# Fourth input-projection chunk of a decoder step computed by seven half-sized products, with the vector engine's work around it laid out anew

## What is computed

```
h = rmsnorm(x)
xin, bg, cg, q, k, v, g_conv, g_attn = split(h @ w_in)     # w_in: 1024 x 6400
y_conv = bg * (causal 3-tap convolution of (cg * xin))
y_attn = attention(rmsnorm(q), rmsnorm(k), v, window 128, bias table, sinks)
x = x + (sigmoid(g_conv)*y_conv + sigmoid(g_attn)*y_attn) @ w_out
x = x + mixture_of_experts(rmsnorm(x))    # top 4 of 32 experts, 1024 x 2048 up and 1024 x 1024 down each
```

## Time and profile before

| | us |
|---|---|
| median of three runs | 1146.74 |
| the profiled execution's own time | 1146.49 |
| span of its trace | 1144.7 |
| PE busy | 1096.0 (96% of the span) |
| VectorE (DVE) busy | 441.5 (39%) |
| VectorE busy from 80 to 100 us | 19.24 of 20 |
| PE idle for DMA, all in the expert stage | 39.9 |

### The profile page before, as it was taken

One profiled execution on the slowest core, in us unless ns is written; L12 is line 12 of the kernel. 1 busy time (PEld: TensorE's weight loads), 2 busy tenths in 40 slices (PEclk: granted clock), 3 DMA queues, 4 the chain that ended last, 5 costly groups with the idle time before them and its releaser, 6 DMA issues.

```text
span 1144.7 us, 15230 instructions
## 1 busy us (share of the span) xinstructions
PE 1096.0 (96%) x6125; PEld 503.9 (44%) x6125; DVE 441.5 (39%) x864; ACT 190.5 (17%) x405; POOL 88.7 (8%) x161
## 2 busy tenths in 40 slices
PE   9999999999999999999899999999999999999997
PEld 6889898543333333333333333333333333333333
DVE  6578786652433323233222222323232323232322
ACT  3233341221321101010101010101010101010101
POOL 1775215000000000000000000000000000000000
PEclk9999999999999999999999999999999999999999
DMA  9937529999999999999999999999999999999996
GB/s 317 320 119 212 184 86 370 418 368 416 402 418 435 415 432 430 435 428 435 427 434 434 428 435 428 435 427 435 434 427 436 428 434 428 435 433 429 427 423 270
DMA packets 53206, 444.38 MB, mean 388 GB/s; under 512 B 13100, under 2 KB 19372, under 8 KB 35740
## 3 DMA queue, kind: packets, MB, share of 16 engines
q1 hardware_dynamic: 46712, 435.83, 91.6%
q0 software_dynamic: 5600, 7.32, 2.4%
q10 hardware_dynamic: 852, 0.64, 0.2%
HBM read 439.78 MB, written 2.37 MB: 386 GB/s over the span
## 4 chain that ended last, share of the span: by engine, by line
PE 62%; DMA 37%; DVE 0%; issue 0%; ACT 0%; ACTq 0%; SPq 0%; DVEq 0%
PE pA L2115 33%; DMA ring<-in_w_up 21%; PE pB L2115 20%; DMA ring<-in_w_down 10%; PE pM L2115 6%; DMA area<-in_w_up 5%; PE pM L2118 1%; PE pA L2118 1%; DMA x<-in_x_prompt 1%; ACT area L1327 0%; DVE x L1961 0%; SPq L848 0%; DVE conv_row L1875 0%; DVE x L2042 0%; ACTq L1109 0%
## 5 line engine op out<-in xcount | busy, mean ns | idle before, releaser
L2115 PE MATMUL pA<-ring,hn 128*64 128x512 f32 x1536 | 352.7, 602 | 23.9 <-DMA ring<-in_w_up 23.8
L2115 PEld LDWEIGHTS pA<-ring,hn 128*64 128x64 f32 x1536 | 105.3, 137 | 219.5 <-issue 185.4
L2115 PE MATMUL pB<-ring,area 128*64 128x512 f32 (+3 forms) x784 | 169.2, 582 | 6.5 <-DMA ring<-in_w_down 5.7
L2115 PE MATMUL pA<-area,hn 128*64 128x512 f32 x512 | 119.3, 609 | 10.4 <-DMA area<-in_w_up 10.4
L2115 PE MATMUL pB<-area,ring 128*128 128x132 f32 (+3 forms) x896 | 119.6, 313 | 0.6 <-DVE tmp L1453 0.5
L2115 PEld LDWEIGHTS pB<-area,ring 128*128 128x128 f32 (+1 forms) x896 | 105.0, 179 | 14.1 <-issue 2.5
L2115 PEld LDWEIGHTS pB<-ring,area 128*64 128x64 f32 (+2 forms) x784 | 58.8, 136 | 98.3 <-issue 85.9
L1961 DVE TENSOR_TENSOR x<-pM,x 128x512 f32<-128x512 f32 x60 | 40.1, 692 | 147.6 <-PE pM L2115 147.6
L1315 ACT ACTIVATE area<-area 128x512 f32<-128x512 f32 x30 | 19.0, 632 | 386.2 <-DVE area L1944 386.2
L1875 DVE COPY conv_row<-pM 128x512 f32<-128x512 f32 x30 | 20.6, 686 | 146.8 <-PE pM L2115 146.8
L2115 PEld LDWEIGHTS pA<-area,hn 128*64 128x64 f32 x512 | 36.0, 139 | 74.5 <-issue 59.5
(11 more groups left out here) (351 smaller groups left out, 918.1 us busy)
## 6 DMA issues: line engine op xcount, KB each, us to landing
ring<-in_w_up SPq DMA_DIRECT2D x36, 4096.0 KB, 29.8
ring<-in_w_down SPq DMA_DIRECT2D x18, 4096.0 KB, 29.2
area<-in_w_up SPq DMA_DIRECT2D x12, 4096.0 KB, 30.2
ring<-in_w_up SPq DMA_DIRECT2D x16, 2048.0 KB, 12.7
area<-in_w_down SPq DMA_DIRECT2D x6, 4096.0 KB, 30.1
ring<-in_w_in SPq DMA_DIRECT2D x22, 1024.0 KB, 9.6
ring<-in_w_down SPq DMA_DIRECT2D x16, 1024.0 KB, 10.2
ring<-in_w_up SPq DMA_DIRECT2D x16, 1024.0 KB, 8.3
```

What stands on the lines that cost most here:

```text
L2115: return pe.matmul(out, w, m, start=start, stop=stop, skip_group_check=True)
```

## The change

Chunk 4 joins `SEVEN`: its four tiles (32 matmuls of 128x264) become seven products (56 matmuls of 128x132). It uses the early activation sums (`EARLY_SIDES`). VectorE gets four more weight sums, and the reads and multiplications of the seven products in place of four tile multiplications; ScalarE one more copy. The multiplication goes into `cx`, with a semaphore of its own, `xin_ready`, for which the first taps wait. The steps around it move: chunk 5's sums stand inside chunk 4, three of them; chunk 6's sums start after slot 5 of chunk 5 and end after slot 2 of chunk 6; unit 0's exponential and scaling stand at slots 0 and 4 of chunk 4; the sample's `s_norm` after slot 6 of chunk 4, its `s_turn` and `s_values` two steps later than before (slots 5 of chunk 5 and 0 of chunk 6); the first four `taps` steps, before at tiles 16 and 17 and twice at slot 0 of chunk 5, stand at slots 0, 0, 1 and 3 of chunk 5; the transpose of the cached keys (`cache_cols`) stands at slot 2 of chunk 2. With one more entry in `RING`, chunks 5, 6 and 7 are loaded one chunk later.

```
-SEVEN = (2, 3, 5, 6, 7, 9, 10, 11, 12)
-EARLY_SIDES = (2, 3, 5)
+SEVEN = (2, 3, 4, 5, 6, 7, 9, 10, 11, 12)
+EARLY_SIDES = (2, 3, 4, 5)
...
-UNIT_STEPS = [(slot(3, 2), slot(3, 4), slot(3, 4), slot(3, 6), slot(3, 6), slot(5, 4), slot(5, 6)),
+UNIT_STEPS = [(slot(3, 2), slot(3, 4), slot(3, 4), slot(4, 0), slot(4, 4), slot(5, 4), slot(5, 6)),
...
-STATE_TAP_STEPS = [14, slot(7, 4)]
-FIRST_TAP_STEPS = [15, 16, 17, 17, 30, 31, 32, 33]
-TAP_STEPS = [16, 17, slot(5, 0), slot(5, 0), 31, 32, 33, slot(9, 0)]
-SIDE_MOVES = [slot(5, 2), slot(5, 4), slot(6, 0)]
+STATE_TAP_STEPS = [slot(4, 4), slot(7, 4)]
+FIRST_TAP_STEPS = [slot(4, 5), slot(4, 5), slot(4, 6), slot(4, 6), 30, 31, 32, 33]
+TAP_STEPS = [slot(5, 0), slot(5, 0), slot(5, 1), slot(5, 3), 31, 32, 33, slot(9, 0)]
+SIDE_MOVES = [slot(5, 2), slot(5, 4), slot(6, 2)]
...
-             5: (14, 15, 17, slot(5, 0)),
-             6: (slot(5, 3), slot(5, 5), slot(6, 0), slot(6, 1)),
+             4: (slot(3, 0), slot(3, 1), slot(3, 2), slot(3, 2)),
+             5: (slot(4, 2), slot(4, 3), slot(4, 5), slot(5, 2)),
+             6: (slot(5, 5), slot(6, 0), slot(6, 1), slot(6, 2)),
...
-    for g, at in enumerate(((slot(2, 1), slot(2, 3), slot(2, 5), slot(2, 6)), (slot(3, 2), slot(3, 3), slot(3, 5), 14))):
+    for g, at in enumerate(((slot(2, 1), slot(2, 3), slot(2, 5), slot(2, 6)), (slot(3, 2), slot(3, 3), slot(3, 5), slot(4, 0)))):
...
-    after[slot(3, 6)].append(("cache_cols", 0))
-    for n, what in ((15, "s_scores"), (16, "s_exp"), (17, "s_norm"), (slot(5, 3), "s_turn"), (slot(5, 5), "s_values")):
+    after[slot(2, 2)].append(("cache_cols", 0))
+    for n, what in ((slot(4, 1), "s_scores"), (slot(4, 2), "s_exp"), (slot(4, 6), "s_norm"), (slot(5, 5), "s_turn"), (slot(6, 0), "s_values")):
...
-                    act.wait_ge(tile_free_dve, DVE_TILES[n] + 1)
+                    if a < 4:
+                        act.wait_ge(xin_ready, 2 if a < 2 else 3)
...
+                factor = cx[:, :, 2:] if xin else yc
...
+                    if xin:
+                        V.tensor_tensor(out, g, out, ALU.mult).then_inc(xin_ready, 1)
+                        dve.wait_ge(xin_ready, ("c22", "c12", "c21").index(name) + 1)
+                        return
```

More of the change, by code:

```diff
@@ L335, in counts @@
             for name in ("r1", "c11", "w", "c22", "c12", "c21"):
-                if name != "c11" or kind == "bg":
+                if name != "c11" or kind in ("bg", "xin"):
                     d += 1
@@ L635, in build @@
         mask_ready = sem("mask_ready")
+        xin_ready = sem("xin_ready")
         ex_in = sem("ex_in")
@@ L1165, in _ @@
                         act.wait_ge(kv_stored, 16 * 16)
-                    n = TILES.index(("xin", 4 if a < 4 else 8, a % 4, a))
-                    act.wait_ge(tile_free_dve, DVE_TILES[n] + 1)
+                    if a < 4:
+                        act.wait_ge(xin_ready, 2 if a < 2 else 3)
+                    else:
+                        act.wait_ge(tile_free_dve, DVE_TILES[TILES.index(("xin", 8, a % 4, a))] + 1)
                     nc.scalar.activation(yc[:, a, 0:SEQ], cx[:, a, 0:SEQ], ACT.Copy,
@@ L1450, in seven @@
                 plain = TILES[2 + 4 * (c - 1)][0] in PLAIN
+                xin = TILES[2 + 4 * (c - 1)][0] == "xin"
+                factor = cx[:, :, 2:] if xin else yc
                 def read(name, out, a, b):
@@ L1461, in times @@
                     dve.wait_ge(tile_free_dve, DVE_READ[c, name])
-                    out = quarter(yc, c, name)
+                    out = quarter(factor, c, name)
+                    if xin:
+                        V.tensor_tensor(out, g, out, ALU.mult).then_inc(xin_ready, 1)
+                        dve.wait_ge(xin_ready, ("c22", "c12", "c21").index(name) + 1)
+                        return
                     link(V.tensor_tensor(out, g, out, ALU.mult))
@@ L1478, in seven @@
                 elif s == 2 and not (gated or plain):
-                    out = quarter(yc, c, "c11")
+                    out = quarter(factor, c, "c11")
                     V.tensor_tensor(out, pairs_of(bank_x), out, ALU.mult).then_inc(tile_free_dve, 1)
```

## The result

The changed kernel took 1155.76 us (median of 6 runs, 1155.52 to 1157.22) against 1146.76 us for the kernel before on the same chip (6 runs, 1146.21 to 1148.07). The ratio is 1.008 with a 95% interval of 1.007 to 1.0091: slower by 9.0 us. The forecast was 1147.3 with a range up to 1149.3, so it was wrong. Its profiled execution took 1155.83 us with a span of 1154.0 us.

The account below looks back on a forecast made before the run. PE bounds the projection, with VectorE nearly bounding it. Narrower products -1.7, old wait gone -0.5, slot 6 of chunk 5 +0.6, slot 1 of chunk 6 +2.15: +0.55 us, 1147.3 us on the median's scale, range 1145.0 to 1149.3.

Parts of the forecast that it names:

- the paragraph on transfers: Unit 0's moves begin near 78.4 us, wanted by the transpose near 91.5; weights have time too: cost nothing.
- The last rival: Unit 0's moves beside chunk 7's weights come late; the transpose waits 1 us or more beyond its slack; chance 0.03.
- the list ahead of sum 1: VectorE's work from `r1` of chunk 5 to chunk 6's sum 1: 16.6 us, done at 99.4 us.
- The clock rival: The pause ahead of slot 1 of chunk 6 drops PE's clock, costing 1.7 us, 1149.0 in all; chance 0.25.
- the wait ahead of slot 1 of chunk 6: PE waits there for chunk 6's weight sum 1: +2.15 us.
- The narrow products: Chunk 4's seven products take less PE time than its four tiles: -1.7 us.
- inside chunk 4: VectorE has 2 us more operations and three sums of chunk 5, yet PE never waits: cost nothing.
- chunk 4's own sums: Four sums of 1.15 us in chunk 3 take 4.6 of VectorE's 6.4 us idle: cost nothing.
- ahead of `r1`: VectorE reaches `r1` of chunk 5 about 0.6 us before PE has finished slot 1.
- the list from the end of `r1`'s wait to `c22`: VectorE's 8.2 us in chunk 5, for which PE waits 0.6 us ahead of slot 6.
- Microseconds of PE here count one for one to the end: In the projection, a shift of PE moves the weight stream's start and the end by the same amount.
- The gain that was said to be there if every wait went: PE keeps up to 2.2 us, 1144.5 us, if VectorE's queue is shorter than counted; chance 0.17.

Follow-up runs that it names:

- e1: The changed kernel with unit 0's exponential and scaling moved back to slot 6 of chunk 3 and slot 0 of chunk 4; 1151.76 us.
- e4: The kernel before with only unit 0's exponential put behind tile 14 and its scaling behind tile 17 of chunk 4; 1155.08 us.
- e7: The changed kernel with chunk 7's weights requested only when unit 0's ten moves have landed; 1153.62 us.
- e3: The changed kernel with unit 0's exponential and scaling early and chunk 6's sum 1 one step earlier (slot 6 of chunk 5); 1149.28 us.
- e8: As e3, plus the sample's values waiting only for the copy of `s_turn`, not for unit 0's values copy; 1146.22 us.
- e6: The changed kernel with throwaway products of 128x264, ten ahead of slot 4 of chunk 5 and five ahead of slot 1 of chunk 6; 1154.8 us.
- e10: As e5, but with unit 0's exponential and scaling late again, as the changed kernel has them; 1151.73 us.
- e5: As e8, plus chunk 5's four sums one place earlier each, all ahead of its slot 0; 1144.77 us.
- e2: The changed kernel with only chunk 6's sum 1 one step earlier (slot 6 of chunk 5 instead of slot 0 of chunk 6); 1155.05 us.

## Why the prediction was wrong

**The step that failed** is the paragraph on transfers: "are wanted by the transpose near 91.5: 5 us to spare ... Cost nothing". Two things in it are false.

- *Who waits.* The transpose reads what the moves write. But unit 1's `bias` writes over what the moves read, and stands in VectorE's queue at 84.4 us, 7 us ahead of the transpose. In the kernel before that wait was there too and never seen, since the moves, started at 72.94 us, had landed near 80.5, 6 us ahead of `bias` at 86.71. I followed the data forward from the moved step and did not list who waits for its source buffer to be free. e1 and e4 show this from both sides: undone, the 4.58 us are gone; with unit 0 late in the kernel before, 4.83 us appear, though there its moves start 8 us later than in the change.
- *How long they take.* "Some 2 to land" was read beside an idle queue. The new place lies beside chunk 7's weights, and they took 5.5 us. The change made both ends of this meeting: the kernel before requested those weights between 60 and 72 us, the changed one near 79. e7 puts 3.0 of the 4.9 us on this. The last rival named exactly these two transfers together and gave them 0.03, because it measured their lateness against the wrong reader. The trace of the kernel before already held the landing time, where unit 1's moves are issued beside another 2 MB of weights (transfers issued from 95 to 106 us):

```profile
ring<-in_w_in SPq DMA_DIRECT2D x2, 1024.0 KB, 7.1
hn<-area POOLq DMA_DIRECT2D x5, 32.0 KB, 5.9
```

**The second false step** is the list ahead of sum 1. It had sum 1 done at 99.4 us by a count of VectorE's operations and 0.15 us of waiting. It was done at about 106.0: 4.92 us for the moves, 1.24 us idle for PE's `s_values`, 0.24 from a later `r1`, and 0.3 of small rest. In the 1.24 us VectorE stands idle between the values copy and its copies of what PE's `s_values` makes, a step that the prediction's list took to be free. Two causes meet there. One is a wait written relative to the last fill, which asks for another copy when the steps are put in another order: e3 and e8 show it, and so does e6, where PE is quick and the list just as long. The other, in the change itself, is PE's first slow stretch, with which it came to `s_values` 0.1 us after that copy had ended. Removing the slow stretch by itself doesn't shorten the list (e6). That removing the wait by itself wouldn't either is read from the change's trace, where PE is free for `s_values` only at 102.81 us, and no run here shows it. I had read such waits for the moved steps by their names, not by what the count comes to in the new order.

**The clock rival** (given 0.25) came true at the place that it named: the clock fell behind the wait ahead of slot 1 of chunk 6. That this wait was 2.14 us, against 2.15 in the forecast, is luck, for both of its ends lay some 7 us later than forecast. Its price was named as 1.7 us and measured 1.66; in e1 and e7 a fall at the same place cost 2.60 and 2.26. The fall behind the wait of 4.58 us was in no rival. That one, 2.70 us long, cost nearly nothing as long as VectorE was behind (e6), and 3.0 us when it wasn't (e10). The Trainium skill, page "TensorE: Matmul & The Clock Gate", section "HAM oscillation — how this bites in real kernels", describes a kernel whose pauses between bursts of matmuls, each longer than 2.14 us, let the clock fall back every time. The fall behind the 4.58 us agrees with it. It says nothing of pauses as short as 2.14 us, behind which the clock fell here, or 2.43 us, behind which in e3 it did not.

**What held.** The narrow products gain 1.50 to 1.64 us (forecast 1.7). No wait arises inside chunk 4, and chunk 4's own sums are hidden. VectorE idles 0.83 us ahead of `r1` (forecast 0.6). With unit 0 early (e3) the list from the end of `r1`'s wait to `c22` takes 8.4 us, 83.89 to 92.29 (forecast 8.2), and PE waits 1.00 us for it (forecast 0.6). Microseconds of PE here count one for one to the end. The gain that was said to be there if every wait went, 2.2 us down to 1144.5, is nearly what e5 reaches, 1144.77, with one wait of 0.72 us left. The mechanism of the gain was right; what was missed was a wait of another kind.

**The sum anew**: +0.55 forecast, +4.92 moves, +1.24 `s_values`, +0.24 and +0.3 small, +1.66 second fall of the clock = +8.9; measured 9.0.

## What to carry to other kernels

When a step is moved later, list every wait that its completion releases, and among them those that wait to overwrite what its transfers read; the first of them in a queue's order, not the reader of the result, sets the slack. Take a small transfer's landing time from a stretch with the same bulk traffic beside it as at its new place. And a wait counted relative to the newest fill changes its meaning whenever steps change places: work out for each which operation it asks for in the new order, since repairing one line here, on top of two other repairs, was worth 1.9 to 3.1 us. Where two engines are late together, removing the delay of one brings nothing, as e6 shows.

## What was unexpected in the hardware

Ten transfers of 32 KB within SBUF, issued at the same pace from POOL's queue, land after 1.8 us alone and after 5.5 us beside 2 MB of weights on SP's queue. The Trainium skill, page "DMA: Bandwidth & Descriptors", section "Queues, rings and completion order", says that each DMA engine takes turns between its queues, a packet at a time; that fits, though no run here shows the turns themselves.

PE's clock fell to the 1.2 GHz level behind waits of 4.58, 4.60, 4.44, 4.83 and, in the change, 2.14 us; not behind 1.57 (e7), 1.80 (e4), nor behind 0.72 and 1.00. It was already down within the wait of 2.14 us in e1 (at 101 to 102 us) and e7 (102 to 103 us), ahead of which lay a wait of 1.30 us and the light 128x8 products. In e2 it fell behind 2.06 us and the same light products, in e6 behind 1.29 us and these, while in e3 2.43 us and these went by without a fall. So the last wait's length does not settle it. A slow stretch cost its full length where PE was what the others waited for (3.0 us in e10), and nearly nothing where VectorE was as late (e6).
